# The norm's reciprocal root stays in the PSUM bank of its sum

## The reference, cut to what matters

```python
def rms_norm(x, g):
    y = xf * lax.rsqrt(jnp.mean(xf * xf, axis=-1, keepdims=True) + EPS)
    return (y * g.astype(jnp.float32)).astype(x.dtype)
```

## Time and profile before

| | |
|---|---|
| median of the timed runs | 2727.14 us |
| the profiled execution, its span | 2724.67 us, 2722.9 us |
| TensorE matmul, weight load | 2523.3 us (93%), 2413.8 us (89%) |
| VectorE, ScalarE, GpSimd | 1106.9 us (41%), 510.8 us (19%), 924.1 us (34%) |
| the eight-tile multiplication, line 1664 | 88 instructions |
| the wide one, line 2016 | 6 instructions, 13.0 us |

### The profile page before, as it was taken

The page is one execution under the profiler, slowest core; times in us unless marked ns, Lnnn a source line. Parts: engine busy times, 40 slices in busy tenths (PEclk is TensorE's granted clock), DMA queues, the critical chain, the costliest instruction groups (busy, mean ns, idle before and its releaser), DMA issues.

```text
span 2722.9 us, 40392 instructions
## 1 busy us (share of the span) xinstructions
PE 2523.3 (93%) x16277; PEld 2413.8 (89%) x16277; DVE 1106.9 (41%) x1685; ACT 510.8 (19%) x1096; POOL 924.1 (34%) x460
## 2 busy tenths in 40 slices
PE   3899977768999999999999789999899999999999
PEld 3899975667999999999999778776899999999998
DVE  6421214645453333333333666623743333333333
ACT  2322113343120000000001434122310000000000
POOL 6333333222323333333334333300233333333332
PEclk9999996889999999999999899979899999999999
DMA  4110131113111111111111310320011111111112
GB/s 174 58 39 32 51 128 36 38 37 130 47 40 47 46 46 46 46 46 46 46 46 47 128 51 32 122 109 1 32 37 47 45 47 45 45 46 46 47 46 75
DMA packets 40994, 154.92 MB, mean 57 GB/s; under 512 B 4784, under 2 KB 11440, under 8 KB 38592
## 3 DMA queue, kind: packets, MB, share of 16 engines
q1 hardware_dynamic: 29760, 107.54, 11.6%
q10 hardware_dynamic: 11136, 45.97, 4.4%
HBM read 135.17 MB, written 18.33 MB: 56 GB/s over the span
## 4 chain that ended last, share of the span: by engine, by line
PE 88%; DVE 8%; ACT 2%; issue 1%; ACTq 0%; DMA 0%; POOL 0%; DVEq 0%; SPq 0%; POOLq 0%
PE bank L576 25%; PE bank L578 25%; PE bank L577 25%; PE bank L770 2%; DVE xt L1664 1%; PE bank L1160 1%; PE bank L1135 1%; PE bank L1155 1%; PE bank L1023 1%; PE bank L1132 1%; PE bank L600 1%; PE bank L655 1%; PE bank L635 1%; PE bank L984 0%; PE bank L643 0%
## 5 line engine op out<-in xcount | busy, mean ns | idle before, releaser
L576 PE MATMUL bank<-x_hi,w_hi 128*128 128x344 f32 (+1 forms) x3304 | 1072.4, 325 | 35.7 <-DVE x_lo L1697 12.5
L577 PE MATMUL bank<-x_lo,w_hi 128*128 128x344 f32 (+1 forms) x3304 | 1058.3, 320 | 0.0
L578 PE MATMUL bank<-x_hi,w_lo 128*128 128x344 f32 (+1 forms) x3304 | 1057.9, 320 | 0.0
L479 POOL TENSOR_TENSOR w_hi<-w_raw,zero 128x1024 fp32r<-128x1024 f32 x187 | 360.9, 1930 | 1534.0 <-PE bank L578 1478.5
L576 PEld LDWEIGHTS bank<-x_hi,w_hi 128*128 128x128 f32 x3304 | 626.6, 190 | 50.8 <-issue 48.0
L577 PEld LDWEIGHTS bank<-x_lo,w_hi 128*128 128x128 f32 x3304 | 625.8, 189 | 1.8 <-issue 0.7
L578 PEld LDWEIGHTS bank<-x_hi,w_lo 128*128 128x128 f32 x3304 | 626.0, 189 | 0.0
L481 POOL TENSOR_TENSOR w_lo<-w_raw,w_hi 128x1024 fp32r<-128x1024 f32 x187 | 461.2, 2466 | 14.7
L1985 DVE TENSOR_TENSOR hid<-sil,bank 128x344 f32<-128x344 f32 x132 | 67.7, 513 | 779.8 <-PE bank L578 742.3
L576 PE MATMUL bank<-hid_hi,w_hi 128*128 128x344 f32 x1056 | 340.1, 322 | 0.0
L577 PE MATMUL bank<-hid_lo,w_hi 128*128 128x344 f32 x1056 | 337.7, 320 | 0.0
(11 more groups left out here) (302 smaller groups left out, 1787.6 us busy)
## 6 DMA issues: line engine op xcount, KB each, us to landing
w_raw<-in_w SPq DMA_DIRECT2D x187, 512.0 KB, 3.4
h<-in_x ACTq DMA_DIRECT2D x3, 1376.0 KB, 15.3
h_spill<-h ACTq DMA_DIRECT2D x1, 4128.0 KB, 11.8
h<-h_spill ACTq DMA_DIRECT2D x1, 4128.0 KB, 13.7
out_y<-h ACTq DMA_DIRECT2D x3, 1376.0 KB, 5.7
g_spill<-ring ACTq DMA_DIRECT2D x6, 516.0 KB, 2.6
h<-in_x ACTq DMA_DIRECT2D x1, 3096.0 KB, 9.9
st_ring<-in_state SPq DMA_DIRECT2D x4, 768.0 KB, 4.3
```

The lines of the kernel that those rows point to most:

```text
L479: nc.gpsimd.tensor_tensor(w_hi[:, s], w_raw[:, s], zero[:].broadcast_to([P, 1024]), ALU.add).then_inc(s_whi, 1)
L576: pe.matmul(out, wh, xh, start=(i == 0), stop=False)
L577: pe.matmul(out, wh, xl, start=False, stop=False)
L578: mm = pe.matmul(out, wl, xh, start=False, stop=(i == n - 1))
```

## The change

The root stays in the bank. ScalarE writes logarithm and exponential back into the bank of the sum, and VectorE's multiplication reads its second operand from there. A table (`NORM_BANK`) gives each norm its bank: 6, 7, 4, 5 for norms 0 to 3, then 6, 7, 6 for 4 to 6, 7, 3, 5 for 7 to 9 and 6, 7, 6 for 10 to 12. A bank is now held until the norm is multiplied, so `norm_sum` waits until the former norm of the same bank has been applied. ScalarE's wait for a free `rstd` buffer goes, and the buffer `rstd_b` too; `rstd` stays for the norms over heads. Two waits of TensorE come in, because norm 2 uses the bank of memory tile 4 and norm 8 that of down tile 21. Waits on the logarithms of norms 2, 3, 8 and 9 before other uses of banks 6 and 7 go.

```diff
+        NORM_BANK = (6, 7, 4, 5, 6, 7, 6, 7, 3, 5, 6, 7, 6)
+        def norm_bank(n, width):
+            return banks[NORM_BANK[n]][:, 0:width]
+        def norm_before(n):
+            return max((m for m in range(n) if NORM_BANK[m] == NORM_BANK[n]), default=None)
...
                 pe.wait_ge(s_fold, n + 1)
-                if n >= 2:
-                    pe.wait_ge(s_ln, n - 1)
+                if norm_before(n) is not None:
+                    pe.wait_ge(s_xt, norm_half(norm_before(n), 1))
                 for k in range(nk):
                     src = sq[:, k, 0:width] if nk > 1 else sq[:, (n - 1) % NCH, 0:width]
-                    mm = pe.matmul(banks[6 + n % 2][:, 0:width], ones, src, start=(k == 0), stop=(k == nk - 1))
+                    mm = pe.matmul(norm_bank(n, width), ones, src, start=(k == 0), stop=(k == nk - 1))
...
                 if t == 5:
+                    pe.wait_ge(s_ev, 5)
                     norm_sum(NORM_A1 + 1, 2, CH)
...
                     if n == 1:
-                        pe.wait_ge(s_ln, NORM_A1 + 2)
...
-                    pe.wait_ge(*((s_vt, m) if m else (s_ln, NORM_A1 + NCH)))
+                    if m:
+                        pe.wait_ge(s_vt, m)
...
                         if last and next_norm and c >= 1:
+                            if c == 2:
+                                pe.wait_ge(s_down, 24 * JFF - 2)
                             norm_sum(next_norm + c - 1, 2, CH)
...
-            def norm_rstd(n, width, out):
+            def norm_rstd(n, width):
                 act.wait_ge(s_sum, n + 1)
-                if n >= 1:
-                    act.wait_ge(s_xt, max(norm_half(n - 2, 1), 1))
-                rstd_of(banks[6 + n % 2][:, 0:width], out[:, n % 2, 0:width], 1.0 / D, s_ln, s_rs, n)
+                rstd_of(norm_bank(n, width), norm_bank(n, width), 1.0 / D, s_ln, s_rs, n)
...
                     op = nc.vector.scalar_tensor_tensor(out=dst[:, k], in0=src[:, k], scalar=gain[:, g0 + k:g0 + k + 1],
-                                                        in1=rs[:, n % 2, 0:w], op0=ALU.mult, op1=ALU.mult)
+                                                        in1=norm_bank(n, w), op0=ALU.mult, op1=ALU.mult)
...
-                    nc.vector.tensor_tensor(xt[:, k], h[:, k, chunk(c)], rstd_b[:, n % 2:n % 2 + 1].broadcast_to([P, HK, CH]), ALU.mult).then_inc(s_xt, 1)
+                    nc.vector.tensor_tensor(xt[:, k], h[:, k, chunk(c)], norm_bank(n, CH).unsqueeze(1).broadcast_to([P, HK, CH]), ALU.mult).then_inc(s_xt, 1)
```

More of the change, by code:

```diff
@@ L213, in trunk_program @@
         rope = at("rope", [P, 2, T], O_L + 8 * ROW)
-        rstd_b = at("rstd_b", [P, 2, CH], O_L + 22016)
         mem_pr = [at("pr_a", [P, H, MEM], O_H + 5 * ROW + 5120), at("pr_b", [P, H, MEM], O_L + 12 * ROW)]
@@ L692, in _ @@
                 if 1 <= n <= len(HEAD_A):
-                    if n == 1:
-                        pe.wait_ge(s_ln, NORM_A1 + 2)
                     head_sum(HN_MK + n - 1, HEAD_A[n - 1][0].shape[1])
@@ L976, in _ @@
                 if 1 <= n <= NB_NORM:
-                    if n == 1:
-                        pe.wait_ge(s_ln, NORM_KV + 2)
                     head_sum(HN_B + n - 1, CH)
@@ L982, in _ @@
                     pe.wait_ge(s_hn, HN_B + n - 1)
-                    pe.wait_ge(*((s_rok, i) if i else (s_ln, NORM_KV + NCH)))
+                    if i:
+                        pe.wait_ge(s_rok, i)
                     pe.matmul(banks[7][:, 0:CH], swap, HEAD_B[n - 2][0], start=True, stop=True).then_inc(s_rsw, 1)
@@ L1225, in _ @@
             square(0, 0, mt[:], MEM)
-            norm_rstd(0, MEM, rstd)
+            norm_rstd(0, MEM)
             act.wait_ge(s_mx0, 1)
@@ L1238, in _ @@
                 if t == 2:
-                    norm_rstd(NORM_A1, CH, rstd_b)
+                    norm_rstd(NORM_A1, CH)
                     act.wait_ge(s_x[1], 16)
@@ L1243, in _ @@
                     norm_hi(NORM_A1, x_hi[:, :, chunk(0)])
-            norm_rstd(NORM_A1 + 1, CH, rstd_b)
+            norm_rstd(NORM_A1 + 1, CH)
             act.wait_ge(s_x[2], 16)
@@ L1338, in _ @@
                 if n == 0:
-                    norm_rstd(NORM_A1 + 2, CH, rstd_b)
+                    norm_rstd(NORM_A1 + 2, CH)
                 if 1 <= n <= len(HEAD_A):
@@ L1503, in norm_after_residual @@
             def norm_after_residual(norm):
-                norm_rstd(norm, CH, rstd)
-                norm_rstd(norm + 1, CH, rstd)
+                norm_rstd(norm, CH)
+                norm_rstd(norm + 1, CH)
                 norm_hi(norm, x_hi[:, :, chunk(0)])
-                norm_rstd(norm + 2, CH, rstd)
+                norm_rstd(norm + 2, CH)
                 norm_hi(norm + 1, x_hi[:, :, chunk(1)])
@@ L1543, in _ @@
             norm_square(0)
-            norm_rstd(NORM_KV, CH, rstd_b)
+            norm_rstd(NORM_KV, CH)
             norm_square(1)
             norm_hi(NORM_KV, x_hi[:, :, chunk(0)])
-            norm_rstd(NORM_KV + 1, CH, rstd_b)
+            norm_rstd(NORM_KV + 1, CH)
             norm_square(2)
@@ L1565, in _ @@
                 if n == 0:
-                    norm_rstd(NORM_KV + 2, CH, rstd_b)
+                    norm_rstd(NORM_KV + 2, CH)
                 if 1 <= n <= NB_NORM:
@@ L1657, in fold, with norm_apply @@
                 nc.vector.tensor_tensor(v[:, 0:2], v[:, 0:2], v[:, 2:4], ALU.add).then_inc(s_fold, 1)
-            def norm_apply(n, src, g0, rs, dst, done=s_xt):
+            def norm_apply(n, src, g0, dst, done=s_xt):
                 w = src.shape[2]
@@ L1674, in norm_lo, with apply_chunk @@
                     nc.vector.tensor_tensor(dst[:, k], src[:, k], hi[:, k].bitcast(F32), ALU.subtract).then_inc(s_lo, 1)
-            def apply_chunk(n, c, g0, rs):
+            def apply_chunk(n, c, g0):
                 if n >= 1:
                     dve.wait_ge(s_lo, norm_half(n - 1, 1))
-                norm_apply(n, h[:, :, chunk(c)], g0, rs, xt)
+                norm_apply(n, h[:, :, chunk(c)], g0, xt)
             def lo_chunk(n, c):
@@ L1692, in _ @@
             fold(0, 0, MEM)
-            norm_apply(0, mt, G_MN, rstd, mem_xt[:, 0], s_mx0)
-            norm_apply(0, mt, G_MN + KT, rstd, mem_xt[:, 1])
+            norm_apply(0, mt, G_MN, mem_xt[:, 0], s_mx0)
+            norm_apply(0, mt, G_MN + KT, mem_xt[:, 1])
             first, second = slice(T - 2 * MEM, T - MEM), slice(T - MEM, T)
@@ L1701, in _ @@
             fold(SQ_A1, NORM_A1, CH)
-            apply_chunk(NORM_A1, 0, G_N1, rstd_b)
+            apply_chunk(NORM_A1, 0, G_N1)
             fold(SQ_A1 + 1, NORM_A1 + 1, CH)
             lo_chunk(NORM_A1, 0)
-            apply_chunk(NORM_A1 + 1, 1, G_N1, rstd_b)
+            apply_chunk(NORM_A1 + 1, 1, G_N1)
             fold(SQ_A1 + 2, NORM_A1 + 2, CH)
@@ L1752, in _ @@
                 if n == 0:
-                    apply_chunk(NORM_A1 + 2, 2, G_N1, rstd_b)
+                    apply_chunk(NORM_A1 + 2, 2, G_N1)
                 if n == 1:
@@ L1967, in swiglu @@
                 for c in range(NCH):
-                    apply_chunk(norm + c, c, g0, rstd)
+                    apply_chunk(norm + c, c, g0)
                     lo_chunk(norm + c, c)
```

## The result

The kernel after takes 2699.91 us (median of 4 runs, 2699.2 to 2700.83), the kernel before 2726.61 us (4 runs, 2725.81 to 2727.68). The ratio is 0.9902, 95% interval 0.9885 to 0.9919. The forecast was 2712.6 us in a range of 2706.5 to 2718.5: the sign was right, the size is outside the range on the fast side. The profiled execution took 2700.17 us with a span of 2698.3 us, 24.6 us shorter than before.

The account below looks back on a forecast made before the run. Matmul time on TensorE was taken to bound the kernel, with VectorE's norm multiplications delayed by turns with GpSimd. Savings of 12.4 + 2.1 = 14.5 us, other terms 0, gave 2712.6 us from 2727.14, range 2706.5 to 2718.5.

Parts of the forecast that it names:

- What bounds the kernel, and who takes turns: TensorE is 88% of the chain; VectorE work on two SBUF operands alternates with GpSimd, work with a bank operand doesn't.
- Rival A: The multiplication still takes turns with GpSimd, its column of gains being a second SBUF operand: 2725 us; chance 0.05.
- Terms 1 and 2: Multiplications without GpSimd turns: norm 0 saves 3.0 us, norms 1 and 2 save 9.4; together 12.4, bounds 7.5 to 20.7.
- the replay: First stage retimed with VectorE's folds and low halves still alternating with GpSimd; put the sum of norm 3 at 75.7 us.
- Rival B: Folds and low halves seldom meet GpSimd once VectorE is ahead: 20.7 + 4.3 us off at most, 2702 to 2708; chance 0.14.
- rival C: The weight split is later than replayed, since GpSimd also loses turns: 7.5 + 0.5 us off, 2719 us; chance 0.12.
- Term 3: Norm ahead of the shared keys, 1516 to 1527 us: chunk 1's multiplication without turns saves 2.1 us, bounds 0.5 to 4.3.
- Term 4: Norms 4 and 10, after the mixers: multiplications uncontended, the third sum's added wait stays under cover of another wait: 0 us.
- rival D: Bank reads bring nothing and the held sums after the mixers lose their cover: 2.6 us slower, 2729.7 us; chance 0.03.
- Term 5: ScalarE's logarithm and exponential now write the bank: 0 us taken, 0.5 us either way over the ten on the path.
- The rule that I weighed and left out: Skill page's fixed VectorE cost, 120 cycles for PSUM against 58 for SBUF: 65 ns per instruction, returning 3.2 us, for 2715.8.
- The last of the signs that I had named: The prediction is wrong if the sum of norm 3 comes as forecast (near 75.7 us) but the end does not follow.

Follow-up runs that it names:

- run 1: The change made for norms 0 to 3 alone, norms 4 to 12 as in the kernel before: 2715.21 us, ratio 0.9969.
- run 2: The change made for norms 7 to 9 alone, the rest as in the kernel before: 2712.82 us, groups 2707.1 to 2713.0 and 2726.1 to 2727.2.
- run 11: The changed kernel with VectorE's four small `sel` casts moved behind the fourth group of window maxima: 2694.27 us, ratio 0.9887.
- run 9: The changed kernel with 1.0 us of useless matmuls ahead of step 32 of the shared projection: 2714.68 us, ratio 0.9955.
- run 6: The kernel before with 3.1 us of useless matmuls ahead of step 32 of the shared projection: 2723.04 us, groups 2714.25 to 2718.23 and 2727.85 to 2733.33.
- run 7: The changed kernel with one useless matmul of 208 columns (0.35 us) ahead of step 32 of the shared projection: 2700.38 us.
- run 4: The changed kernel with five more squares of the memory tokens on ScalarE (about 1.95 us each) ahead of norm 0: 2706.44 us.
- run 12: The kernel before with the four `sel` casts moved behind the fourth group of window maxima: 2709.14 us, groups 2704.1 to 2709.1 and 2716.6 to 2723.0.
- run 5: The kernel before with three useless matmuls (1.7 us together) ahead of layer A's last feed-forward step: 2729.62 us.
- run 3: The changed kernel's banks and TensorE waits, but the root written to and read from SBUF as in the kernel before: 2726.22 us, ratio 1.0.
- run 10: The kernel before with 2.4 us of useless matmuls ahead of step 32 of the shared projection: 2724.17 us, groups 2717.34 to 2719.92 and 2728.43 to 2733.19.
- run 8: The kernel before with 1.0 us of useless matmuls ahead of step 32 of the shared projection: 2729.64 us.

## Why the prediction was right and where it failed

**What bounds the kernel, and who takes turns: right.** Line 1866's evidence carried over: 88 instructions with an SBUF tensor, an SBUF column of gains and a bank stay within 475 to 481 and 560 to 573 ns, beside a GpSimd as busy as before. Rival A is out by that row.

**Terms 1 and 2, 12.4 us: the replay was right.** The 16 instructions of norm 0 were to take 6.2 us, and take 6.36 (VectorE's timeline):
```profile
21.76 6.36 DVE L1671 SCALAR_TENSOR_TENSOR mem_xt<-mt,gain,bank 128x256 f32<-128x256 f32 x16 [3.03 <-ACT bank L1201]
```
The sum of norm 3 was to start at 75.7 and starts at 75.88, 12.2 us earlier than before. Tile 7's evacuation was to end at 65.6 and ends at 65.55 + 0.38 = 65.93. Norm 2 was to be multiplied at 66.6, and is at 66.86; the first row is norm 1:
```profile
42.76 3.95 DVE L1671 SCALAR_TENSOR_TENSOR xt<-h,gain,bank 128x344 f32<-128x344 f32 x8 [7.68 <-ACT bank L1201]
...
66.86 3.95 DVE L1671 SCALAR_TENSOR_TENSOR xt<-h,gain,bank 128x344 f32<-128x344 f32 x8 [8.11 <-ACT bank L1201]
...
70.73 2.16 DVE L1662 TENSOR_TENSOR sq<-sq 128x1376 f32<-128x1376 f32 x1
...
72.93 2.90 DVE L1664 TENSOR_TENSOR sq<-sq 128x688 f32<-128x688 f32 x1
```
Two errors cancel within it: unit 7's low half is ready at 61.00, where I had 62.4, and tile 7 then takes 4.55 us, where I had 2.45, since its first products run 0.21 us apart after the wait and the last 0.12 (the chain has both). Rival B (20.7 us) and rival C (7.5 us) are both out at this place: the folds do take turns, and the split is not later than replayed. Of the 12.2 us, 11.3 are left at 233 us. Around and behind the sum of norm 3 TensorE's granted clock averages 0.82 (75 to 92 us), against 0.89 in the kernel before (88 to 104 us), so some of the lead may go there; but one pair of traces does not settle a microsecond. The first `ring` starts at 232.6 to 234.0 us in the five traces with the new norms 1 to 3 and no work added ahead of it, and at 244.1 to 246.2 in the eight with the old ones, of which the kernel before's is the earliest: the means are 12.0 us apart. Run 1 confirms the two terms alone (10.9 us in its trace).

**Term 3, 2.1 us: too small.** The pair of chunk 1 starts at 1506.33 where it was 1516.57, and the sum of norm 9 at 1514.51 where it was 1527.55: 10.2 us of lead have become 13.0, and behind the stage 13.3. So 2.8 us at the sum and 3.1 in all (3.3 in run 2). VectorE's timeline:
```profile
1506.33 3.09 DVE L2023 TENSOR_TENSOR xt<-h,bank 128x1376 f32<-128x1376 f32 x2
...
1509.34 2.63 DVE L1662 TENSOR_TENSOR sq<-sq 128x1376 f32<-128x1376 f32 x1
...
1512.01 2.45 DVE L1664 TENSOR_TENSOR sq<-sq 128x688 f32<-128x688 f32 x1
```
The pair takes 3.09 us (forecast 3.2). The fold ends 8.1 us after the pair's start instead of 8.8 (25.4 - 16.57). The piece that differs is GpSimd's gain multiplication between the two steps:
```profile
1510.48 3.25 POOL L556 TENSOR_TENSOR w_raw<-w_raw,gain 128x1024 f32<-128x1024 f32 x1
```
It ends 7.4 us after the pair's start (1513.73 - 1506.33), where the replay had 24.6 - 16.57 = 8.0. So the turns were there, the first of them to 0.1 us, and one was mis-sized by 0.6 us. The gain of 3.1 us does not all reach the windowed attention: from the last `pr_b` to the first `pw` the kernel after takes 98.9 us and the one before 97.1. In that stretch lies the dip of the clock named under run 11, 6.8 us long after and 3.4 before, which by an estimate accounts for 1.7 us: 3.4 us more at half clock.

**Term 4, 0 us: right, through the cover that rival D doubted.** The held third sum is the last of TensorE's sums before layer A's feed-forward part:
```profile
742.51 1.48 PE L601 MATMUL bank<-sq,cst 128*128 128x344 f32 x2 [2.87 <-DVE xt L1671]
744.01 0.62 PE L584 MATMUL bank<-x_hi,w_hi 128*128 128x344 f32 x1
```
The sum was to take 1.33 us and takes 1.48. It waits for the multiplication (`<-DVE xt`), ends at 743.99, and the first product starts at 744.01, which is 10.1 us earlier than before (754.11): the lead it came with. The cover was all used up, and held.

**Term 5, 0 us: the size is a small gain.** ScalarE's logarithm (L1199) and exponential (L1201), in the view by source:
```profile
L1199 ACT ACTIVATE bank<-bank x13: 368/442/452, 21.0 to 1940.2; 128x344 f32<-128x344 f32 x12, 128x256 f32<-128x256 f32 x1
...
L1201 ACT ACTIVATE bank<-bank x13: 368/442/442, 21.4 to 1940.7; 128x344 f32<-128x344 f32 x12, 128x256 f32<-128x256 f32 x1
...
L1201 ACT ACTIVATE rstd<-rstd x40: 418/492/497, 84.7 to 1700.8; 128x344 f32<-128x344 f32 x36, 128x256 f32<-128x256 f32 x4
```
The exponential takes 442 ns from bank to bank, 492 ns from SBUF to SBUF; the logarithm takes 442 ns where it took 457. Some 65 ns a norm, 0.65 us over the ten on the path, beside my bound of 0.5; no run shows this gain by itself. The Trainium skill ("ScalarE: Activation LUTs", "Step-by-step: what each stage is for") has PSUM as ScalarE's quicker destination; the trace agrees, with 15 ns for the destination of the logarithm and 50 ns for source and destination of the exponential.

**The rule that I weighed and left out.** The fixed cost by which a bank source would add 65 ns is not there: 567 ns with the bank, 569 without, 476 against 473 ns at 256 columns. The trace does not agree with the Trainium skill's page ("VectorE: DVE Perf Modes", "The TRN2 errata").

**The step that failed.** It is the last sentence of terms 1 and 2, "From there TensorE has work without a gap, and the gain stays", and the sum's silence on all stages that the change does not touch. I priced the matmul stages as if each kept the clock of the trace before. One did not: the windowed attention ran its first 34 us at half clock in the kernel before, which the page's clock row and the windows view would have told me, and 12 us earlier it runs at full clock. The sum should have held a term of 0 or some 13 us with a chance beside it. No case of mine reached 2700 us; rival B, 2702 to 2708, came nearest, for a wrong reason. The last of the signs that I had named is the one that came: the sum of norm 3 as forecast, and the end not following.

How far this is shown: with the whole change in place and 1.0 us added (run 9), the time is 2714.68, that is 2713.7 without the added work, against 2726.3 of the kernel before, both at the low clock: 12.6 us. At the high clock it is 2699.9 against 2713.5 to 2716.5, which the kernel before took in the three executions named under run 6: 14 to 17 us. My 14.5 us lies between. What decides between the clocks is not shown. The work just ahead is no answer. Up to the fall, the 22 us of the kernel before, of the one after and of run 9 are these:
```profile
1776.00:1798.00 22.00, 19.90 (x208) 14.27 (x199) 11.04 (x20) 7.47 (x17) 0.00 (x0) 1.00 0.37 145
```
```profile
1764.40:1786.40 22.00, 19.90 (x213) 14.27 (x205) 11.04 (x20) 7.47 (x17) 0.00 (x0) 1.00 0.37 145
```
```profile
1766.90:1788.90 22.00, 19.89 (x207) 14.26 (x197) 11.02 (x20) 7.46 (x17) 0.00 (x0) 1.00 0.37 145
```
TensorE's matmuls and weight loads, VectorE and ScalarE agree to 0.02 us in busy time, and the clock is full in each; behind them it falls in the first and the third and not in the second. Small shifts count: 1.0 us more took the clock away (run 9) and 0.35 us did not (run 7). But the time since the span's start does not sort the traces. With the new norms 1 to 3 the first `pw` starts at 1779.1 (run 11), 1787.1 (after), 1789.1 (run 7) and 1789.8 us (run 4) with the high clock, and at 1789.0 (run 1) and 1789.4 (run 9) with the low one. With the old ones it starts at 1795.7 (run 12), 1799.9 (run 2) and 1804.8 (run 6) with the high clock, and at 1798.6 (before), 1799.3 (run 5), 1800.2 (run 3), 1801.2 (run 10) and 1802.5 (run 8) with the low one.

The expectation of run 9 counts from instants at which the clock can change. I had carried them on from changes seen nearby; no run shows such instants. A sign that I had read out of the traces missed in run 7, this one hit in run 9, and run 10, sent to the high side by it, was low in five executions of ten. A rival stands beside it, the dip of the clock between 1729 and 1752 us. Where it lasts 6.5 us or more (after, runs 2, 4 and 7) the clock is high later; where it lasts some 3.4 us it is low later in six traces of seven (before, runs 1, 3, 5, 9 and 10; run 6 is high); of the three without a dip run 8 is low and runs 11 and 12 are high. Run 9 moved the stage and halved the dip at once, so it does not tell the two apart. The cause stays open.

## What to carry to other kernels

An operand left in PSUM takes a VectorE instruction out of its turns with GpSimd, and costs nothing in itself here; replay the stage with the pieces that still take turns, since they are what is late next. Before summing, ask the granted clock of every stage that will only move in time: where a busy TensorE stands at half clock, a shift of a microsecond can be worth more than the change. And judge a change of less than that with both kernels at the same clock, by adding a little useless work to either, or a kernel will be credited with luck. Here 13 of the 26.7 us were luck of this kind.

## What the runs showed of the hardware that I had not expected

- TensorE stayed at 1.2 GHz for some 34 us while its records cover all of the time (36.00 of 36.00 us, 170 matmuls, clock 0.53). Records of matmuls overlap, so this says that it never stood still, not that it worked at its peak. The Trainium skill ("TensorE: Matmul & The Clock Gate", "Part 1: The HAM clock gate") has a busy engine come to its full clock after a short while, and puts the loss at under 1% of a typical kernel; the trace does not agree on the first and agrees on the second (14.4 of 2727 us).
- The same program takes either clock from one execution to the next (runs 2, 6, 10, 12, and the kernel before in 3 executions of 69), as the times and the mean granted clocks show.
- Four casts of 4 x 128 elements took 6.11 us beside GpSimd's copies and 0.61 us elsewhere (run 11).
- The stretch around the gated attention has two lengths some 4 us apart (375.3 to 375.5 and 378.5 to 380.6 us), whichever the kernel; why stays open.
